# Joints of a tuned Hawk/NSA decoder kernel: the samples' chain, a late third of columns, the norm's inversion and a weight split moved

## The reference

```
x = x + m[:, gate] * rmsnorm(o, g_out)                    # residual, sandwich norm
h = rmsnorm(x, g_in) * (1.0 + m[:, scale]) + m[:, shift]  # next stage's input
z = h @ w_in                                              # its first product
rmsnorm(x) = x * rsqrt(mean(x * x, axis=-1) + 1e-6)
```

## Time and profile before

| | |
|---|---|
| median of 3 runs | 3140.73 us (3139.68 to 3142.48) |
| profiled execution, its own time | 3141.2 us |
| its span | 3139.2 us, 57788 instructions |
| mean granted clock of TensorE | 0.989 of 2.4 GHz |
| busy: PE, DVE, ACT, POOL | 96%, 63%, 28%, 37% |
| a tile of 72 products | 11.47 us |

### The profile page before, as it was taken

The page is one execution under the profiler, slowest core; times in us unless marked ns, Lnnn a source line. Parts: engine busy times, 40 slices in busy tenths (PEclk is TensorE's granted clock), DMA queues, the critical chain, the costliest instruction groups (busy, mean ns, idle before and its releaser), DMA issues.

```text
span 3139.2 us, 57788 instructions
## 1 busy us (share of the span) xinstructions
PE 3028.0 (96%) x23209; PEld 2802.9 (89%) x23209; DVE 1965.5 (63%) x3566; ACT 863.6 (28%) x1362; POOL 1164.5 (37%) x790
## 2 busy tenths in 40 slices
PE   5999999999999999999979999999999999999997
PEld 4998999999999999899856666777999999999997
DVE  5667386657584856856477777402287658585676
ACT  5555231101010101302238888502231101010101
POOL 1332324434344443134116565301324444444443
PEclk9999999999999999999999999999999999999998
DMA  5222322222222212322564010275221111111113
GB/s 217 86 78 100 126 107 91 72 74 75 68 81 63 73 47 92 136 74 79 163 217 156 2 41 2 74 256 198 67 87 48 44 44 48 47 48 48 48 47 119
DMA packets 78197, 277.98 MB, mean 89 GB/s; under 512 B 9035, under 2 KB 19539, under 8 KB 74723
## 3 DMA queue, kind: packets, MB, share of 16 engines
q1 hardware_dynamic: 75362, 256.83, 24.5%
q10 hardware_dynamic: 2592, 17.73, 1.7%
HBM read 247.54 MB, written 36.27 MB: 90 GB/s over the span
## 4 chain that ended last, share of the span: by engine, by line
PE 82%; issue 6%; DVE 5%; ACT 3%; SPq 2%; POOL 1%; DVEq 1%; DMA 1%; POOLq 1%; ACTq 0%
PE PA L2223 33%; PE PB L2223 32%; PE PA L1342 2%; PE PB L1527 2%; PE PCD L1355 2%; PE PB L1366 1%; PE PA L2314 1%; PE PCD L290 1%; PE PB L2314 1%; DVE ring L1428 1%; PE PA L1366 1%; ACT ring L1398 1%; POOL ring L1479 1%; ACT pt L1391 1%; SPq L1779 1%
## 5 line engine op out<-in xcount | busy, mean ns | idle before, releaser
L1965 POOL TENSOR_TENSOR w_hi<-w_raw,misc 128x1024 fp32r<-128x1024 f32 x187 | 372.3, 1991 | 1501.7 <-PE PA L2223 620.3
L1967 POOL TENSOR_TENSOR w_lo<-w_raw,w_hi 128x1024 fp32r<-128x1024 f32 x187 | 545.3, 2916 | 26.9 <-issue 0.4
L2223 PE MATMUL PA<-hB_hi,w_hi 128*128 128x348 f32 x1272 | 273.6, 323 | 0.0
L2223 PE MATMUL PB<-hB_hi,w_hi 128*128 128x348 f32 x1272 | 272.3, 322 | 0.0
L2223 PE MATMUL PA<-hB_hi,w_lo 128*128 128x348 f32 x1272 | 271.5, 322 | 0.0
L2223 PE MATMUL PB<-hB_hi,w_lo 128*128 128x348 f32 x1272 | 271.5, 322 | 0.0
L2223 PE MATMUL PA<-hB_lo,w_hi 128*128 128x348 f32 x1272 | 271.0, 321 | 0.0
L2223 PE MATMUL PB<-hB_lo,w_hi 128*128 128x348 f32 x1272 | 271.0, 321 | 0.0
L2223 PEld LDWEIGHTS PA<-hB_hi,w_hi 128*128 128x128 f32 x1272 | 215.0, 189 | 0.4
L2223 PEld LDWEIGHTS PB<-hB_hi,w_hi 128*128 128x128 f32 x1272 | 215.0, 188 | 0.4
L2223 PEld LDWEIGHTS PB<-hB_lo,w_hi 128*128 128x128 f32 x1272 | 215.1, 188 | 0.0
(11 more groups left out here) (677 smaller groups left out, 6635.8 us busy)
## 6 DMA issues: line engine op xcount, KB each, us to landing
w_raw<-in_w SPq DMA_DIRECT2D x196, 512.0 KB, 3.7
mt<-in_mw SPq DMA_DIRECT2D x32, 1024.0 KB, 5.1
pages<-in_pages SPq DMA_DIRECT2D x64, 384.0 KB, 4.0
x_dram<-X SPq DMA_DIRECT2D x12, 1032.0 KB, 3.9
X<-x_dram SPq DMA_DIRECT2D x3, 4128.0 KB, 12.5
mt_even<-in_mw SPq DMA_DIRECT2D x8, 1024.0 KB, 5.4
mt_odd<-in_mw SPq DMA_DIRECT2D x8, 1024.0 KB, 5.0
vall<-in_pages_v SPq DMA_DIRECT2D x64, 128.0 KB, 2.6
```

Of the source, the lines that this page charges most:

```text
L1965: pool.tensor_tensor(hi, raw, zero.broadcast_to([P, 1024]), ALU.add)
L1967: pool.tensor_tensor(lo, raw, hi.bitcast(F32), ALU.subtract).then_inc(sem("w_split"), 1)
L2223: mm = pe.matmul(PS[ps][:, c, 0:width], w[:, w0:w0 + P], x[:, k, c * width:(c + 1) * width], start=(k == 0 and n == 0), stop=(k == K - 1 a ...
```

## The change

- `stats`: fewer warming products, 5, 10, 5, 6 for 8, 12, 8, 8 ahead of the sums and 16 for 20 behind the transposes; `rms_spread` is signalled after the samples' transpose and after the last.
- `residual`: the third tile's low part goes; two copies of shifts take its place; the samples' chain moves from ahead of row 0 to behind row 1, with the samples' high columns; the rows are weighted and added one after the other.
- `norm_tiles`: rows 0 and 1 are multiplied in the first two thirds only, the last third of both once `edge_hi` has come. The norm's root is turned into eight columns by two transposes (`turn`), inverted, and spread by eight transposes.
- `lo_rows`: waits for the turn, inverts 8 columns instead of 256, and ends with the third tile's low part. GpSimd waits for that before its next split. SyncE's code is not touched.

```diff
@@ stats
-        warm(pe, PC, {1: 8, 3: 12, 5: 8, 7: 8}[n])
+        warm(pe, PC, {1: 5, 3: 10, 5: 5, 7: 6}[n])
...
-                if c in (3, 7):
+                if c in (KT, 7):
                     mm.then_inc(sem("rms_spread"), 1)
-            warm(pe, PA[:, 1, :], {1: 20, 3: 20, 5: 20}[n])
+            warm(pe, PA[:, 1, :], 16)
@@ lo_rows
-        root = NB[NREG[n]][f"t0_{NREG[n]}"][:, 0:256]
+        turned = PC[:, 256:512].rearrange("p (h q x) -> p h q x", h=2, q=4)[:, :, :, 0]
         for k in range(KT):
             lo_row(dve, hn, scale, k)
             if k == 3:
-                dve.wait_ge(sem("sqrt_done"), n + 1)
-                dve.reciprocal(root, root)
+                dve.wait_ge(sem("rms_spread2"), n - 1)
+                dve.reciprocal(rst[:, 0:KT].rearrange("p (q h) -> p h q", h=2), turned)
                 dve.reciprocal(rms[:, NPR:TOK], rms[:, NPR:TOK]).then_inc(sem("rms_inverted"), 1)
+        first_lo(dve, n - 1, 2)
@@ norm_act
-        act.wait_ge(sem("rms_spread2"), n // 2)
+        act.wait_ge(sem("rms_spread2"), n)
@@ first_splits
             for i in (0, *range(3, n)):
+                if i == 3:
+                    pool.wait_ge(sem("w_split"), t0 + 3)
@@ norm_tiles
             for k in range(KT):
                 pe.wait_ge(sem("hi_done"), 8 * hn + k + 1)
-                if k == 0:
+                for b in range(2):
+                    terms(b, k, hi_pairs, k == 0, False, (0, 1) if k < 2 else range(NCH))
+                if k == 1:
                     pe.wait_ge(sem("edge_hi"), hn if hn < 4 else 4)
-                for b in range(2):
-                    terms(b, k, ((w_hi, HB[0]), (w_lo, HB[0])), k == 0, False)
+                    for b in range(2):
+                        for early in range(2):
+                            terms(b, early, hi_pairs, early == 0, False, (2,))
...
+            def turn():
+                pe.wait_ge(sem("sqrt_done"), n + 1)
+                for half in range(2):
+                    mm = pe.transpose(PC[:, (2 + half) * P:(3 + half) * P], root[:, half * P:(half + 1) * P], ident)
+                mm.then_inc(sem("rms_spread2"), 1)
+
             def spread():
                 pe.wait_ge(sem("rms_inverted"), n // 2)
-                for q in range(4):
-                    mm = pe.matmul(PCD[q // 2][:, q % 2 * 256:q % 2 * 256 + 256], ident[:, 32 * q:32 * q + 1].broadcast_to([P, P]),
-                                   root[:, 0:256], start=True, stop=True, skip_group_check=True)
+                for c in range(KT):
+                    mm = pe.transpose(PCD[c // 4][:, c % 4 * P:(c % 4 + 1) * P], rst[:, c:c + 1].broadcast_to([P, P]), ident)
...
-                if (k, b) == (3, 1):
+                if (k, b) == (1, 1):
+                    turn()
+                if (k, b) == (4, 1):
                     spread()
@@ residual
             dve.reciprocal(rst, rst).then_inc(sem("rst_ready"), 1)
-            first_lo(dve, n, 2)
+            dve.tensor_copy(HB[0][:, :, WIDE - 3:WIDE], mrows(shift)[:, :, 0:3])
+            dve.tensor_copy(HB[0][:, :, TOK:TOK + NC], mrows(shift))
             dve.wait_ge(sem("x_back"), (16, 32, 48, 64)[r])
...
+            def samples():
+                dve.wait_ge(sem("rms_spread"), n)
+                normed_samples(src, PB[:, 2, P - NS:P])
+                dve.tensor_tensor(ts, ts, msamp(gate), ALU.mult)
+                dve.drain()
+                dve.tensor_tensor(X[:, :, NPR:TOK], X[:, :, NPR:TOK], ts, ALU.add)
+                dve.drain()
+                dve.tensor_tensor(ts, X[:, :, NPR:TOK], msamp(scale), ALU.mult)
+                dve.drain()
+                dve.tensor_copy(HB[0][:, :, NPR:TOK], ts).then_inc(sem("edge_hi"), 1)
...
             dve.wait_ge(sem("row_out"), n + 1)
-            weighted(1)
-            dve.drain()
-            for k in range(2, KT + 1):
-                if k < KT:
-                    weighted(k)
-                added(k - 1)
-                dve.drain()
+            for k in range(1, KT):
+                weighted(k)
+                dve.drain()
+                added(k)
+                if k == 1:
+                    samples()
```

More of the change, by code:

```diff
@@ L2309, in norm_tiles, with terms @@
                 after(pe, sem("ev_act"), evicted + b)
-            def terms(b, k, pairs, first, last):
+            hi_pairs = ((w_hi, HB[0]), (w_lo, HB[0]))
+            def terms(b, k, pairs, first, last, thirds=range(NCH)):
                 for i, (w, x) in enumerate(pairs):
-                    for c in range(NCH):
+                    for c in thirds:
                         mm = pe.matmul(PS[(p0 + b) % 2][:, c, 0:CW], w[(t + b) % 2][:, k * P:(k + 1) * P],
@@ L2589, in first_rows, with residual @@
             dve.drain()
-        def residual(r, n, src, gate, scale=None, shift=None):
+        def residual(r, n, src, gate, scale, shift):
             b = NB[NREG[n]]
@@ L2596, in residual @@
             dve.reciprocal(rst, rst).then_inc(sem("rst_ready"), 1)
-            first_lo(dve, n, 2)
+            dve.tensor_copy(HB[0][:, :, WIDE - 3:WIDE], mrows(shift)[:, :, 0:3])
+            dve.tensor_copy(HB[0][:, :, TOK:TOK + NC], mrows(shift))
             dve.wait_ge(sem("x_back"), (16, 32, 48, 64)[r])
-            dve.wait_ge(sem("rms_spread"), n)
-            normed_samples(src, PB[:, 2, P - NS:P])
-            dve.tensor_tensor(ts, ts, msamp(gate), ALU.mult)
-            dve.drain()
-            dve.tensor_tensor(X[:, :, NPR:TOK], X[:, :, NPR:TOK], ts, ALU.add)
+            def samples():
[8 more added lines that the diff above has]
+                dve.tensor_copy(HB[0][:, :, NPR:TOK], ts).then_inc(sem("edge_hi"), 1)
             def weighted(k):
@@ L2615, in residual @@
             added(0)
-            if scale is not None:
-                dve.tensor_tensor(ts, X[:, :, NPR:TOK], msamp(scale), ALU.mult)
+            dve.wait_ge(sem("row_out"), n + 1)
+            for k in range(1, KT):
+                weighted(k)
                 dve.drain()
-                edge_hi(dve, shift)
-            dve.wait_ge(sem("row_out"), n + 1)
-            weighted(1)
-            dve.drain()
-            for k in range(2, KT + 1):
-                if k < KT:
-                    weighted(k)
-                added(k - 1)
-                dve.drain()
[L2628 to L2636, removed]
+                added(k)
+                if k == 1:
+                    samples()
+            dve.tensor_tensor(HB[1][:, :, NPR:TOK], ts, HB[0][:, :, NPR:TOK].bitcast(F32), ALU.subtract)
+            dve.tensor_copy(HB[1][:, :, WIDE - 3:WIDE], mrows(shift)[:, :, 0:3])
+            dve.tensor_tensor(HB[1][:, :, TOK:TOK + NC], mrows(shift), HB[0][:, :, TOK:TOK + NC].bitcast(F32), ALU.subtract)
+            dve.drain()
+            dve.tensor_tensor(ts, X[:, :, NPR:TOK], X[:, :, NPR:TOK], ALU.mult)
+            dve.drain()
+            dve.tensor_reduce(rms[:, NPR:TOK], ts.rearrange("p k s -> p s k"), AXX, ALU.add).then_inc(sem("edge_lo"), 1)
+            dve.drain()
         def last_out(n):
```

## The result

| | before | after |
|---|---|---|
| median | 3140.2 us (3138.78 to 3142.48, 4 runs) | 3170.23 us (3167.23 to 3173.39, 4 runs) |
| ratio | | 1.0094 [1.0081, 1.0106] |
| span of the profiled execution | 3139.2 us | 3164.9 us, own time 3167.2 |
| mean granted clock | 0.989 | 0.984 |

The change costs 30.0 us; 28 had been forecast, within 3158 to 3180.

The account below looks back on a forecast made before the run. TensorE, busy for 96% of the span, was taken as the bound, so gaps count. Two stalls, clock loss and the second joint's gain: 12.4 + 13.5 + 3.0 - 0.9 = +28.0 us, giving 3169, range 3158 to 3180.

Parts of the forecast that it names:

- SyncE's queue order: In first and third joints, stores of X queue behind a load awaiting the late low part; third tile 12.4, 13.5 later.
- T: End of the third tile's low part on VectorE: 420.5 us in the first joint, 2307.4 in the third.
- The landing: From the late low part's end until weights and X have landed: 13.8 us, bounds 12.5 and 17.7.
- Rival 1: The stall, with stores as slow as in the second joint, 17.7 for 13.8 us twice: 3177, chance 0.15.
- The third joint: Its third tile starts at 2322.4 us instead of 2308.9, 13.5 later.
- The clock: TensorE at half clock for 3.4 us behind each stall, losing 1.5; twice, 3.0 us, bounds 0 and 6.
- First part of a joint: Up to the third row's products: gains 1.1 us in the first joint, 0.6 in the third, 0.8 in the second.
- W: Start of a joint's first weighted row: 384.4 us for 384.93 in the first joint, 0.5 gained; third joint 0.
- Low products: On TensorE's path, turn and eight transposes replace the 1.73 us spread of the norm: net gain 0.1 us.
- Second joint: Its stores stood behind a later load anyway, so no stall; only a gain of 0.9 us.
- Rival 2: No stall, as stores are not behind the load or their landing is covered; only gains stand: 3138, chance 0.07.
- Rival 3: No stall, but fewer warming products let the clock fall inside the joints, 3 x 1.5 us: 3142, chance 0.03.

Follow-up runs that it names:

- e2: Kernel before with only the third tile's low part moved behind the low rows, with GpSimd's wait: 3172.44 us, ratio 1.0104.
- e1: Kernel after with SyncE issuing the four stores of X ahead of the weight load, the first store waiting for edge_hi: 3139.66 us, ratio 0.9997.
- e4: Kernel after with two of the four stores of X ahead of the weight load, two behind it: 3161.08 us, ratio 1.0066.
- e7: Kernel after with 58 more warming products on TensorE in the third joint's stall alone: 3167.36 us, ratio 1.0081.
- e3: Kernel after with the low part early again, no wait of GpSimd, first store waiting for edge_hi: 3142.01 us, ratio 1.0004.
- e6: e1 with the warming counts of the kernel before (8, 12, 8, 8 and 20): 3138.35 us, ratio 0.9994.
- e10: The same kernel as e6, run and profiled once more: 3140.5 us, ratio 0.9997.
- e8: Kernel after with the stores of X behind one more weight load, tile_load(t0 + 5): 3180.44 us, ratio 1.0125.

## Why the prediction was right

**SyncE's queue order.** Right, and it is the change's whole loss (e2 alone, and e1 without it). Forecast stores behind 420 and 2307 us; they stand at 420.15 and 2318.83 us, the latter with the 12 us gathered before.

**T.** Forecast 420.5, measured 419.76, near by luck. From the part sums to the end of the low rows it takes 7.66 us against 7.64 before, so the wait for the turn costs nothing where I had 0.4. The joint also began 1.09 us earlier, and the half clock under the transposes took 0.98 back; neither was in the forecast.

**The landing.** This term was mis-sized: 13.8 forecast, 15.0 measured in the first joint (419.76 to 434.75) and 14.2 in the third, inside my bounds of 12.5 and 17.7. I took one transfer of X plus a share for the weights; e4 shows that in its place the data moves at 423 GB/s and 3.8 us are fixed, with a load and four stores in a row. Third tile 435.96 against 435.5, since T was early. Rival 1 (3177) was not needed.

By the Trainium skill (DMA: Bandwidth & Descriptors), with about 358 GB/s (Specifications) and 2.0 us fixed (Anatomy of one DMA — SWDGE (gpsimd) path, which gives it for transfers issued by GpSimd), the same landing would be 15.3 us and the total 3172, both estimates and both close to what was measured. The trace agrees with the total but not with its parts: the rate between e4 and the kernel after (423 and 460 GB/s in the two joints) lies near the page's 435 GB/s and the fixed part is nearly twice the page's, so the sum is close because the two errors cancel. My remark that 12.5 us for 4.23 MB lies between the page's two rates holds only with its fixed 2.0 us counted in; without them the row gives 338 GB/s, below both.

**The third joint.** 12.96 later within the joint for 13.5.

**The clock.** 1.4 a stall (13.10 and 13.07 for 11.71 and 11.68) for 1.5, and e7 gives it back in the third joint. Half clock stood from the first product, 435.96 us, to about 439.1 us, 3.1 us; I had said 3.4.

**First part of a joint.** Row 2's products at W + 6.4 and row 3's at W + 10.1, forecast 6.3 and 10.3; the gain from W on is 0.77 for 0.6. The 0.5 ahead of W is right at equal clock, but it comes from the samples' chain: with the transposes at full clock W is 6.31 before and 5.81 to 5.83 in every kernel with the chain moved, wherever the low part stands (e1 and e3) and with either count of warming products (e6), against 6.13 with the low part alone moved (e2). In the kernel after it can't be seen, since its transposes ran at half clock and cost 0.98: W is 6.80 from the start of the joint. That W stood at 384.33 us, where I had 384.4, is luck, as the joint began 1.09 early. The forecast had no term for the clock ahead of W.

**Low products.** Gain 0.43 for 0.1: the turn takes 0.23 us of the chain, not 0.4, and the spread 1.04, my 1.15.

**Second joint.** 0.80 shorter for 0.9, but in other parts: 1.20 gained from W on (0.77 and 0.43), and W 0.40 later, of which 0.32 is the later start of its transposes.

**Covered work.** `fst` went at 434.81 us and VectorE's first convolution stayed hidden, as said.

**Rival 2, no stall.** Its condition was tried in e1 and its price, 3138, was 1.7 under what 11 runs gave (3139.66, before 3140.36). Its joints' gain is real (4.0 us for my 2.8), but the stage behind took 1.6 of it back. Rival 3 fell as a forecast, since there was a stall. Its mechanism is open: e1 with the fewer warming products has joints of 42.81, 44.37 and 42.72 us, e10 with the old counts 42.79, 44.34 and 43.02, but half clock under the first joint's transposes is more frequent among the profiles with fewer (four of seven, one of six).

## What to carry to other kernels

When an instruction moves on one engine, follow the semaphore it signals into every in-order queue: here a weight load waited for it, and transfers that had nothing to do with it stood behind that load; the first of them moved by 28 us. Put a transfer that many wait for ahead of a load that waits for late work, and then check what its old place had guaranteed (here the stores were behind the samples' columns by accident). Measure a gain of a few us in the stage that has it, because untouched stages may differ by as much between close variants.

## What the hardware showed unexpectedly

- Four stores of 1032 KB behind one load of 512 KB: 5.0 us for 2064 KB of them, 423 GB/s, and 3.8 us that do not scale (after and e4, first joint; 460 GB/s and 3.8 us in the third).
- A TensorE idle stretch of 14.6 us cost 1.4 us of products at half clock behind it; 116 warming products in such a stretch, 13.11 us, took all of it back. The cost does not follow the idle time: 9.6 us idle made the third tile 13.74 us (e4), 19.2 us idle 14.20 (e8), for 11.71 at full clock.
- The clock before the second joint differs from run to run over the same products: granted 0.96 over 1205 to 1245 us before, in e1 and in e10, 1.00 in the others, e6 among them, which is the same kernel as e10; 1.4 us of time.
- Two profiles of one kernel (e6 and e10) differ by 1.03 us in W of the second joint: eight transposes took 1.04 us at full clock and 1.91 at half.
- VectorE's inversion: 256 columns took 1.75 us before, 8 columns 0.21.
- The granted clock over the same 92 us of attention chunks was 0.89 to 0.96 in kernels that differ only elsewhere, and their end moved by 5.3 us with it.
